# Preparing the first pair of recurrence heads beside the even layer's attention, with the low-rank projections first

## What is computed

```python
p = centred_shift(pa, prm['mu_prev'], prm['mu_next'])
r, k, v, wl, al, gl = jnp.split(p, A_SPLITS, axis=-1)
w_raw = prm['w0'] + jnp.einsum('bsdl,dlc->bsdc', jnp.tanh(wl), prm['w2'])
decay = jnp.exp(-jnp.exp(-jax.nn.softplus(-w_raw) - 0.5))
iclr = jax.nn.sigmoid(prm['a0'] + jnp.einsum('bsdl,dlc->bsdc', al, prm['a2']))
kk = k * prm['k_k'];  kk = kk / jnp.maximum(jnp.sqrt(jnp.sum(kk * kk, -1)), 1e-12)
k_dir = k[:, :, None, :] * (1 + (iclr - 1) * prm['k_a'])
```

## Time and profile before

| | us |
|---|---|
| median of 3 runs (lowest to highest) | 2042.5 (2041.62 to 2043.52) |
| the profiled execution | 2046.16 |
| its span | 2044.3 |
| PE busy | 1821.5 (89%) |
| DVE busy | 1100.9 (54%) |
| ACT busy | 881.3 (43%) |
| POOL busy | 254.9 (12%) |

### The profile page before, as it was taken

One profiled execution on the slowest core, in us unless ns is written; L12 is line 12 of the kernel. 1 busy time (PEld: TensorE's weight loads), 2 busy tenths in 40 slices (PEclk: granted clock), 3 DMA queues, 4 the chain that ended last, 5 costly groups with the idle time before them and its releaser, 6 DMA issues.

```text
span 2044.3 us, 39320 instructions
## 1 busy us (share of the span) xinstructions
PE 1821.5 (89%) x16658; PEld 1505.3 (74%) x16658; DVE 1100.9 (54%) x1631; ACT 881.3 (43%) x1397; POOL 254.9 (12%) x236
## 2 busy tenths in 40 slices
PE   4899879889888889999998998799978998879997
PEld 1776558777677678888887766698867676669985
DVE  1457564465545554324436866565455476556863
ACT  2326544344332444223325266465342266546652
POOL 0100034525253000000001100110010000000210
PEclk9999989999998989999999999899989999979999
DMA  8342233222231223233233411365535432435542
GB/s 275 95 124 85 83 126 102 86 88 85 85 106 64 83 83 103 83 103 103 83 103 89 134 57 42 103 186 185 185 113 168 163 101 98 132 115 169 183 162 105
DMA packets 201372, 237.13 MB, mean 116 GB/s; under 512 B 14347, under 2 KB 158573, under 8 KB 201197
## 3 DMA queue, kind: packets, MB, share of 16 engines
q1 hardware_dynamic: 195856, 227.33, 34.9%
q10 hardware_dynamic: 5341, 7.30, 1.1%
HBM read 233.56 MB, written 1.05 MB: 115 GB/s over the span
## 4 chain that ended last, share of the span: by engine, by line
PE 74%; DVE 10%; ACT 8%; POOL 3%; issue 2%; DMA 2%; ACTq 1%; SPq 0%; DVEq 0%; POOLq 0%
PE bank L1499 17%; PE bank L1501 17%; PE bank L1500 17%; PE bank L1691 9%; ACT window L2564 2%; DVE window L1995 2%; PE bank L1679 2%; PE bank L1658 2%; DMA arena<-in_w_ada 2%; PE bank L1670 1%; PE bank L1550 1%; ACT arena L2625 1%; PE bank L1698 1%; PE bank L1876 1%; PE bank L1564 1%
## 5 line engine op out<-in xcount | busy, mean ns | idle before, releaser
L1501 PE MATMUL bank<-window 128*128 128x512 f32 (+1 forms) x1988 | 687.2, 346 | 0.0
L1499 PE MATMUL bank<-window 128*128 128x512 f32 (+1 forms) x1716 | 620.0, 361 | 57.8 <-POOL window L2981 40.0
L1500 PE MATMUL bank<-window 128*128 128x512 f32 (+1 forms) x1880 | 670.9, 357 | 0.0
L1499 PEld LDWEIGHTS bank<-window 128*128 128x128 f32 x1716 | 334.1, 195 | 115.0 <-issue 35.1
L1501 PEld LDWEIGHTS bank<-window 128*128 128x128 f32 x1988 | 385.0, 194 | 45.2
L1500 PEld LDWEIGHTS bank<-window 128*128 128x128 f32 x1880 | 366.0, 195 | 47.7 <-issue 0.5
L1995 DVE TENSOR_TENSOR window<-arena,window 128x2048 fp32r<-128x2048 f32 (+1 forms) x132 | 297.4, 2253 | 190.3 <-ACT window L2564 188.7
L2564 ACT ACTIVATE window<-arena 128x2048 fp32r<-128x2048 f32 (+3 forms) x260 | 316.7, 1218 | 168.4 <-DMA arena<-in_w_ff 51.1
L2564 ACT ACTIVATE arena<-bank 128x256 f32<-128x256 f32 (+1 forms) x262 | 113.5, 433 | 365.8 <-PE bank L1501 132.1
L1691 PE MATMUL bank<-arena 64*64 64x64 f32 (+1 forms) x5888 | 217.1, 229 | 24.2 <-DVE arena L1485 11.0
L1691 PEld LDWEIGHTS bank<-arena 64*64 64x64 f32 x5888 | 204.9, 139 | 45.3 <-issue 15.5
(11 more groups left out here) (298 smaller groups left out, 2097.2 us busy)
## 6 DMA issues: line engine op xcount, KB each, us to landing
arena<-in_w_ff SPq DMA_DIRECT2D x64, 1024.0 KB, 5.4
arena<-in_w_ada SPq DMA_DIRECT2D x48, 1024.0 KB, 5.4
arena<-in_w_in SPq DMA_DIRECT2D x23, 1024.0 KB, 5.0
arena<-in_w_ffn_up SPq DMA_DIRECT2D x22, 1024.0 KB, 5.1
arena<-in_w_ffn_down SPq DMA_DIRECT2D x10, 1024.0 KB, 5.1
arena<-in_w_in_even SPq DMA_DIRECT2D x9, 1024.0 KB, 5.5
arena<-in_w_out SPq DMA_DIRECT2D x8, 1024.0 KB, 5.1
arena<-in_w_in_odd SPq DMA_DIRECT2D x8, 1024.0 KB, 5.2
```

The lines of the kernel that those rows point to most:

```text
L1499: e.matmul(o, rr(l[0]), rr(r[0]), start=start, stop=False)
L1500: e.matmul(o, rr(l[0]), rr(r[1]), start=False, stop=False)
L1501: return e.matmul(o, rr(l[1]), rr(r[0]), start=False, stop=stop)
```

## The change

- Blocks of the recurrence's projection are made in the order 12, 13, 14, 4, 5, 8, 9, 0, 1, 2, 3, 6, 7, 10, 11. The gates (tanh and sigmoid of blocks 12 and 14, L2669 and L2671) follow block 14 at once.
- A fourth generator `begun` runs beside the attention. Once blocks 4, 8, 12, 13, 14 are projected (round 6), it takes eleven steps of `prepare(0)`, one a round: squares, sums, norm, two rounds of reciprocals, turning v, low-rank products of direction 0, decay, exponentials, scaling, and in round 16 the low-rank products of direction 1. It stands before `modulation` in each round.
- After the stage, pair 0 needs only its last two products for direction 0 (`rotated`, which now waits for the stage), then direction 1 from its decay on.
- The buffers of the preparation lie in the area of the hidden rows `H`, free since the norm, and above the attention's. The two low-rank weight tables and the scan mask are loaded before the stage (`lora weights`); five tables are left in `recurrence_start`.

```diff
     def a_proj():
-        for j in range(15):
+        for j in (12, 13, 14, 4, 5, 8, 9, 0, 1, 2, 3, 6, 7, 10, 11):
             if j % 2 == 0:
                 cols(("pA", j // 2), W_e, j * 128, min(256, 1920 - j * 128))
             take("pA", j)
             step("pA", j)
             give("pA", j)
-            yield
-        step("pA gates")
+            projected.add(j)
+            yield
+            if j == 14:
+                step("pA gates")
...
+    projected, prepared = set(), set()
+    h_cols = [arena[:, h_at + 512 * i:h_at + 512 * i + 512] for i in range(8)]
+    kb, sg, cu, ex, kk, w2s, a2s, scanm = h_cols
+    BE0, KA0, VB0 = [sb(512) for _ in range(2)], [sb(512) for _ in range(2)], sb(8, 64)
+    step("lora weights")
...
         for d in range(2):
-            take("w", p, d)
-            take("a", p, d)
-            step("prep lora", p, d)
-            give("w", p, d)
-            give("a", p, d)
-            yield
+            if p or not d:
+                prep_lora(p, d)
+                yield
             step("prep decay", p, d)
             yield
             step("prep exps", p, d)
             yield
             step("prep scale", p, d)
             yield
+            if not p and not d:
+                prep_lora(p, 1)
+                yield
             step("prep last", p, d)
...
+    def begun():
+        while not projected >= {4, 8, 12, 13, 14}:
+            yield
+        for _ in range(11):
+            next(now)
+            yield
+
+    run(a_proj(), b_rotate(), begun(), slowed(modulation(0, 8, 16)))
...
     def rotated(e, q, p, d):
         ar = AR[p % 2][d]
-        q.wait_ge(q.last(), at("exps", p, d))
+        q.wait_ge(q.last(), at("exps", p, d), *(() if p else stage("even")))
...
+        def lora_weights():
+            sp.wait_ge(*prep_free(0))
+            load(landed_lora, at("lora consts"),
+                 [(w2s, I["a_w2"][0].rearrange("d l c -> (d l) c")), (a2s, I["a_a2"][0].rearrange("d l c -> (d l) c")), (scanm, C["scanm"])])
+
         def recurrence_start():
             sp.wait_ge(*stage("even"))
             load(landed_units, at("recurrence consts"),
-                 [(w2s, I["a_w2"][0].rearrange("d l c -> (d l) c")), (a2s, I["a_a2"][0].rearrange("d l c -> (d l) c")),
-                  (g2s, I["a_g2"][0]), (scanm, C["scanm"]), (lvl, C["lvl"]), (lvl0, C["lvl0"]), (tri, C["tri"]), (id2, C["id2"])])
+                 [(g2s, I["a_g2"][0]), (lvl, C["lvl"]), (lvl0, C["lvl0"]), (tri, C["tri"]), (id2, C["id2"])])
```

More of the change, by code:

```diff
@@ L727, in program, with prepare, prep_lora @@
     sets["B"] = Attention(items, [at("swapped", "kB"), at("wmask"), at("vB")], more_p)
-    run(a_proj(), b_rotate(), slowed(modulation(0, 8, 16)))
+    projected, prepared = set(), set()
+    h_cols = [arena[:, h_at + 512 * i:h_at + 512 * i + 512] for i in range(8)]
+    kb, sg, cu, ex, kk, w2s, a2s, scanm = h_cols
+    BE0, KA0, VB0 = [sb(512) for _ in range(2)], [sb(512) for _ in range(2)], sb(8, 64)
+    PC, ka1 = sb(2, 8), sb(4)
+    step("lora weights")
+    def prepare(p):
+        step("prep squares", p)
+        yield
+        take("kk sums", p)
+        step("prep sums", p)
+        yield
+        give("kk sums", p)
+        step("prep norm", p)
+        yield
+        for i in range(4):
+            step("prep recip", p, i)
+            if i % 2:
+                yield
+        for q in range(2):
+            take("v turned", p, q)
+            step("prep v", p, q)
+            give("v turned", p, q)
+        yield
+        for d in range(2):
+            if p or not d:
+                prep_lora(p, d)
+                yield
+            step("prep decay", p, d)
+            yield
+            step("prep exps", p, d)
+            yield
+            step("prep scale", p, d)
+            yield
+            if not p and not d:
+                prep_lora(p, 1)
+                yield
+            step("prep last", p, d)
+            prepared.add((p, d))
+            yield
+        step("prep rk", p)
+        yield
+        take("bonus", p)
+        step("prep bonus", p)
+        give("bonus", p)
+    def prep_lora(p, d):
+        take("w", p, d)
+        take("a", p, d)
+        step("prep lora", p, d)
+        give("w", p, d)
+        give("a", p, d)
+    now = prepare(0)
+    def begun():
+        while not projected >= {4, 8, 12, 13, 14}:
+            yield
+        for _ in range(11):
+            next(now)
+            yield
+    run(a_proj(), b_rotate(), begun(), slowed(modulation(0, 8, 16)))
     step("end", "even")
@@ L736, in program @@
     del live[2:]
-    spare = [(xt_at, xt_at + 8192), (ring_top - 4096, high_top), (gb_at, gb_at + 2048), (h_at, h_at + 4096)]
+    spare = [(xt_at, xt_at + 8192), (ring_top - 4096, high_top), (gb_at, gb_at + 2048)]
     def spare_or_new(*shape):
@@ L767, in program @@
     AR = [[spare_or_new(2, 512) for _ in range(2)], [a.rearrange("p (a b) -> p a b", a=2) for a in wide[0:2]]]
-    BE = [[spare_or_new(512) for _ in range(2)], [wide[2][:, 0:512], wide[2][:, 512:1024]]]
-    KA = [[spare_or_new(512) for _ in range(2)] for _ in range(2)]
-    VB = [spare_or_new(8, 64) for _ in range(2)]
+    BE = [BE0, [wide[2][:, 0:512], wide[2][:, 512:1024]]]
+    KA = [KA0, [spare_or_new(512) for _ in range(2)]]
+    VB = [VB0, spare_or_new(8, 64)]
     ET, FF, RT = [[[sb(8, 64) for _ in range(2)] for _ in range(2)] for _ in range(3)]
-    kb, sg, cu, ex, kk = [spare_or_new(512) for _ in range(5)]
-    w2s, a2s, scanm = [spare_or_new(512) for _ in range(3)]
     g2s = sb(512)
     lvl, lvl0, tri, id2 = spare_or_new(2, 6, 64), spare_or_new(2, 2, 64), spare_or_new(2, 2, 64), spare_or_new(64)
-    PC = spare_or_new(2, 8)
     Zb = extra[:, 3072:3328].rearrange("p (a b c) -> p a b c", a=2, b=2)
-    ka1 = spare_or_new(4)
     PNs = [sb(2, 8) for _ in range(4)]
@@ L784, in program @@
     lane_of, lane_free, first_of = {}, [None] * LANES, {}
-    prepared, finished, chained = set(), set(), set()
+    finished, chained = set(), set()
     order = [[4, 5, 6, 7, 0, 1, 2, 3], [7, 6, 5, 4, 3, 2, 1, 0]]
@@ L841, in lane @@
             lane_free[n] = u
-    def prepare(p):
-        step("prep squares", p)
-        yield
-        take("kk sums", p)
-        step("prep sums", p)
-        yield
[L849 to L861, removed]
-            take("w", p, d)
-            take("a", p, d)
-            step("prep lora", p, d)
-            give("w", p, d)
-            give("a", p, d)
[L867 to L881, removed]
     def preparing(first):
@@ L925, in program @@
     pending = []
-    now = prepare(0)
     while (0, 0) not in prepared:
@@ L1454, in prep_free @@
     def prep_free(p):
-        return stage("even") if p < 2 else units_of(p - 2)
+        return stage("even") if p == 1 else units_of(p - 2) if p else [at("scaled rows", "m0", k, q) for k in range(4) for q in (0, 4)]
     def prep_before(p, d):
-        return [at("prepared", p, 0)] if d else [at("prepared", p - 1, 1)] if p else stage("even")
+        return [at("prepared", p, 0)] if d else [at("prepared", p - 1, 1)] if p else prep_free(0)
     def keys(e, q, p, d):
@@ L1772, in prep_lora @@
             s, w, a = slice(64 * d, 64 * d + 64), bank("w", p, d), bank("a", p, d)
-            pe.wait_ge(w.before, at("recurrence consts"), at("pA gates"))
+            pe.wait_ge(w.before, at("lora consts"), at("pA gates"))
             e.matmul(w.b[:, :], w2s[s, p * 128:p * 128 + 128], pA[s, 12, :], start=True, stop=True).then_inc(*pe.tick(w.full))
@@ L2178, in values @@
                 e.tensor_copy(it["close"], u.b[:, 0:256]).then_inc(*ve.tick(u.empty))
-        def recurrence_start():
-            ve.wait_ge(ve.last(), *stage("even"))
+        def lora_weights():
+            ve.wait_ge(ve.last(), at("vc 1"))
             e.tensor_scalar(ka1, col("a_k_a", 0, 4), -1.0, 1.0, MUL, ADD).then_inc(*ve.tick())
@@ L2540, in vector @@
                  "even start": even_start, "qB": qB_, "vB": vB_, "sink": sink, "pA": pA_, "rotate": rotate_, "swap": swap_,
-                 "round masks": round_masks, "round caus": round_caus, "scores": scores, "scale p": scale_p, "values": values, "recurrence start": recurrence_start,
+                 "round masks": round_masks, "round caus": round_caus, "scores": scores, "scale p": scale_p, "values": values, "lora weights": lora_weights,
                  "unit grams": unit_grams, "unit tlt": unit_tlt,
@@ L2732, in prep_squares @@
         def prep_squares(p):
-            sc.wait_ge(sc.last(), *prep_free(p), *([at("bonus", p - 1)] if p else []))
+            sc.wait_ge(sc.last(), at("pA", 4 + p), *prep_free(p), *([at("bonus", p - 1)] if p else []))
             e.activation(sg, pA[:, 4 + p, :], ACT.Square, scale=col("a_k_k", p)).then_inc(*sc.tick(at("kk squares", p)))
@@ L3025, in gpsimd @@
                 steps[name](*a)
-    landed_first, landed_columns, landed_h, landed_even, landed_units, landed_odd, landed_bias, landed_ret, landed_second, landed_decay, stored = [
```

(5 more changed lines are left out.)

1 line of the change is left out of this document (added).

## The result

| | before | after |
|---|---|---|
| median, us | 2043.0 (4 runs, 2041.6 to 2047.7) | 2072.8 (4 runs, 2066.6 to 2076.9) |
| profiled execution, us | 2046.16 | 2076.26 |
| its span, us | 2044.3 | 2074.4 |

The change makes the kernel slower: ratio 1.0139, 95% interval 1.0104 to 1.0174, or +28 us; the medians are 29.8 apart. The forecast was +29.3, 2072.

The account below looks back on a forecast made before the run. PE was taken to bound the even stage, and a chain of short ACT and DVE operations the head behind it. Stage 0.2 + 1.9 + 39.4 + 10.2 = 51.7 us longer, head 22.4 less: +29.3, 2072 us, range 2052 to 2088.

Parts of the forecast that it names:

- The late splits: Even stage, rounds 4 to 14: PE waits for six splits directly ahead of their use, 39.4 us, bounds 32 and 45.
- the upper bound: Late splits in the even stage: 45 us if table reloads and reciprocals in rounds 9 to 13 count in full.
- The clock: Even stage: PE resumes below full speed after each of six stalls, 10.2 us lost, bounds 0 to 14.7.
- PE's added work: Even stage: round 12's low-rank step adds 1.9 us to PE; without stalls all added products show, 5.8 us.
- The head: From the stage's end to direction 1's grams: 17.5 us in place of 39.9, gain 22.4, bounds 18 and 26.
- Nothing in that piece changes: Head, from direction 1's scan to its grams: 9.9 us as before, as its operations and the exp table stay.
- first grams at a clock above 0.50: Just behind the stage: a sign expected in the trace, with the first grams within 2 us of the stage's end.
- The gain taken whole: Recurrence: the head's 22.4 us counted in full, since pairs 1 to 3 are prepared behind direction 1's start.
- The splits are in time: Rival, even stage: preparation simply hidden, stage grows 0.2 + 5.8, head shrinks 22.4; -16.4, 2026 us; chance 0.11.
- The rival's condition: Even stage: the six stalls and their clock cost must fall from 49.6 below about 16 us for a gain.
- The preparation is in the way: Rival, even stage: one more 2 us in each of rounds 7 to 13, about +12 on top, 2084; chance 0.12.
- The gain is lost: Rival, behind the stage: PE draws set the recurrence's end, only the stage's growth stays, +52, 2094; chance 0.07.

Follow-up runs that it names:

- the order alone: The kernel before with the new order of blocks and early gates, without preparation beside the attention; 2086.6 us, ratio 1.0208.
- the one with the generator shifted: The changed kernel, block 14 still third, with the conditioning generator starting one round later; 2030.0 us, ratio 0.9933 to the kernel before.
- the one with three late splits: The kernel with kept pairs, but block 14 projected ninth, so only rounds 10, 12 and 14 make chunks late; 2054.9 us, ratio 1.0062.
- The warm kernel: The changed kernel with four added PE products ahead of the projections of blocks 4, 8, 0, 2, 6 and 10; 2065.2 us, ratio 1.0103.
- kept pairs: The changed kernel with block 14 projected last instead of third, so chunks are made in odd rounds again; 2026.1 us, ratio 0.9913.
- one round later: The kernel with kept pairs plus one idle turn of the preparing generator, nothing else; 2034.6 us, ratio 0.9957 to the kernel before.
- early decay with kept rounds: Kept pairs with direction 1's decay step first, then one idle turn so later preparation steps keep their rounds; 2029.7 us, ratio 0.9933.

## Why the prediction was right, point by point

- **The late splits (39.4 us).** Right in place, kind and sum. The waits were 4.75, 4.75, 8.67, 7.46, 5.72 and 7.73, 39.1 in all. The forecast's 39.4 was net of the old 1.6 us stall, so it is 1.9 us above what was found (37.5). Each of the six is within 1 us. Round 8 was sized at 9.6, which is what the order alone gives (9.5); with the preparation it is 8.7. Round 10 was too low at 6.5: with the order alone the waits of rounds 10 and 14 are 5.4 and 5.9, with the preparation 7.5 and 7.7, so what the preparation puts ahead of a split costs some 2 us there. For round 14 that was in the sum. For round 10 it was left to the upper bound: a table load of 1.28 us stands in ACT's queue at 197.67 that the kernel with the order alone doesn't have there; the reciprocals on DVE were done before ACT's half of the split. The kernel with the order alone, the one with the generator shifted and the one with three late splits show the cause from three sides.
- **The clock (10.2 us).** Right in kind, a little small. The warm kernel shows 7 to 8 us of it, with three of six stalls not filled, and the order alone leaves some 12. The stage grew by 57.5 us in the profiled executions, 1.5 of it already there before the first projection. Of the other 56.0, 37.5 are waits and about 6 are PE's own added products. That leaves some 12 us for the clock and small waits together, as with the order alone. The forecast had 51.7 for the stage, 5.8 too little.
- **PE's added work (1.9 us shown, the rest inside stalls).** The kernel with kept pairs, which has no such stalls, ends its stage at 256.4, 10.6 later than before (0.9 of it already there before the first projection); the 5.8 us of products are the larger part.
- **The head (22.4 us less).** Direction 1's start came 20.1 us nearer to the stage's end (39.9 to 19.7 with rounding). The tables landed 1.2 us sooner than assumed; but from the scan to the grams it took 13.3 us and not 9.9. "Nothing in that piece changes" was the wrong step. The operations stayed, but DVE keeps the plan's order and now stood idle in the middle of them for 2.90 us, for lane 0's matmuls (318.25). These stood behind the conditioning chunk, and PE had waited 3.41 us for its transfer (312.81), which SP issues behind the tables. With kept pairs the two waits are 2.23 and 3.28; in the kernel before there is neither. On top of that the same scan took 1.63 in place of 1.23 and the tensor-scalar operation 1.37 in place of 0.55, beside POOL's masks. This is read from the traces; no run takes it apart. Also "first grams at a clock above 0.50" was wrong: 64 matmuls took 4.53 us, as before.
- **The gain taken whole.** The forecast let nothing happen after direction 1's start. The traces show otherwise: 37.4 us behind at that point, 32.8 at the end of the recurrence. Those 4.6 us come from within the recurrence, whose steps of preparation now stand one round earlier against the lanes. Two kernels that differ in this shift alone are 9 us apart. In the profiled executions it took 373.5 to 375.1 us from the first grams to the end of the recurrence with the old places (before, the order alone, one round later), and 367.9 to 371.5 in four of the five kernels with the new ones; the slow execution of kept pairs took 374.7. The prediction had noted that lane 0 would be one step less advanced, and took it as a possible loss. Whether an earlier direction 1 by itself shortens the recurrence is not shown: in the kernels that brought it forward by 2 us and more all later steps moved too.
- **The number is in part luck.** The stage came out 5.8 us longer than forecast and the head's gain 2.3 smaller, which makes 37.4 in place of 29.3. That the measured difference is 29.8 all the same (30.1 in the profiled executions) is due to the 4.6 us above, which were in no term, and to 2.7 us in the rest, where both kernels run the same steps and executions scatter.
- **The rivals.** "The splits are in time" gave 2026 at a chance of 0.11; the kernels in which they are in time measured 2026.1 and 2030.0. The rival's condition wasn't met, and its number is right with wrong parts too. With kept pairs the stage grew by 10.6 and not 6.0, and direction 1's last product ends 10.1 us earlier than before (275.52 against 285.62), where the rival had 16.4; the shifted round makes up for it. "The preparation is in the way" is refuted by kept pairs: the same steps, no stalls on attention's lines over 2 us. What there is of it are the 2 us each that rounds 10 and 14 gained. "The gain is lost" would be 2094; the changed kernel is 14 us under the one with the order alone, not 22. The profiled spans differ by 10.2, and the changed kernel also carries the preparation in its stage (it ends 13.5 us later than with the order alone), so the difference isn't the head alone.

## What to carry to other kernels

When work is issued in the order of a plan, look at what keeps the plan's places: here a split stands where the chunk before it was made, and one block on its own in a pair shifted six of them from a whole round ahead to directly ahead of their use. The sums of busy time show nothing of it (DVE did the same 102 us in 202 us of stage and in 156); comparing, in the old trace, the time at which the consumer will be ready with the time at which a step in the new place ends predicts the stalls within 1 us each. And compare a forecast with the trace at every landmark between its terms, not only at the end: here two errors and an effect that nobody had planned cancelled. The best median is that of the changed kernel with block 14 projected last, 0.87% under the kernel before; the shifted generator and the early decay with kept rounds can't be told from it.

## What the runs showed of the hardware

- An operation of DVE can take longer beside one of POOL. The same tensor-scalar of 128x512 took 0.55 us in the kernel before, with POOL idle, and 1.37 in the changed one (312.52), where one of POOL's masks ran at the same time:

```profile
278.87 0.55 DVE L2253 TENSOR_SCALAR arena<-arena 128x512 f32<-128x512 f32 x1
```
```profile
312.02 1.60 POOL L2989 TENSOR_TENSOR arena<-arena 128x512 f32<-128x512 f32 x1
```

  Not every one does: the two masks on DVE at 308.34 and 309.06 took 0.69 us each beside POOL's of 308.34 to 310.34.

- The clock behind a wait of one and the same length differs from run to run. PE waits 2.8 us for the split of round 9 in five kernels with the same order of blocks; the first matmul then took 0.80, 0.79 and 0.70 us in three of them and 0.50 in two.

- Executions of one kernel scatter, and their mean granted clock with them. The kernel before ran in 2035.7 us at a mean clock of 0.955 and in 2054.0 at 0.944; the one with the idle turn in 2022.0 at 0.962, with eleven others between 2032.7 and 2037.0 at 0.948 to 0.954. Differences under some 5 us need the many runs that stand behind the ratios here.
